# Attention loads moved from ScalarE to SyncE, through DRAM tables laid out in the projections

## The reference

```
k_rows = lax.dynamic_slice_in_dim(kg, rs, kh, axis=1)[:, :, col_idx]   # 8 rows x 32 columns
bias   = jnp.take(bias_c, dr_idx, axis=1)                              # relative position, per head
s_loc  = einsum('bjqhd,bijkhd->bhjqik', q_r, k_rows) + bias            # NEG_BIG outside the window
s_ctx  = einsum('bjqhd,bmhd->bhjqm', q_r, ctx_k)                       # 256 cached context keys
p      = softmax(concatenate([s_loc, s_ctx], axis=-1))
o      = einsum(p_loc, v_rows) + einsum(p_ctx, ctx_v)
```

## Time and profile before

| what | value |
|---|---|
| device time, three runs | 3695.7, 3701.32, 3702.32 us, median 3701.32 |
| profiled execution | 3698.1 us, span 3696.4 us |
| granted clock of TensorE, mean over the span | 0.866 |
| busy TensorE, weight loads | 3125.3 us, 2724.5 us |
| busy VectorE, ScalarE, GpSimd | 1934.6, 1164.2, 654.8 us |
| DMA | 497.80 MB, mean 135 GB/s |

### The profile page before, as it was taken

The page is one execution under the profiler, slowest core; times in us unless marked ns, Lnnn a source line. Parts: engine busy times, 40 slices in busy tenths (PEclk is TensorE's granted clock), DMA queues, the critical chain, the costliest instruction groups (busy, mean ns, idle before and its releaser), DMA issues. The chain is left out here.

```text
span 3696.4 us, 52649 instructions
## 1 busy us (share of the span) xinstructions
PE 3125.3 (85%) x19831; PEld 2724.5 (74%) x19831; DVE 1934.6 (52%) x4013; ACT 1164.2 (31%) x2012; POOL 654.8 (18%) x900
## 2 busy tenths in 40 slices
PE   8679999975887788898689942999999999999990
PEld 1367788864666677787568832999999999999990
DVE  3531213224444488788534457566666566666644
ACT  0531224311333322222123301344444444444422
POOL 3013400014444100022101100012111111211102
PEclk9689999996889766557689955999999999999995
DMA  7334522216777210111133323556655555665528
GB/s 273 127 109 149 172 73 89 76 57 140 151 158 153 89 51 29 52 44 37 42 103 116 113 115 105 171 181 185 197 175 180 183 183 183 185 197 175 177 81 313
DMA packets 350119, 497.80 MB, mean 135 GB/s; under 512 B 98403, under 2 KB 239755, under 8 KB 348397
## 3 DMA queue, kind: packets, MB, share of 16 engines
q1 hardware_dynamic: 251615, 376.04, 31.2%
q0 software_dynamic: 24336, 85.48, 8.2%
q10 hardware_dynamic: 74000, 34.10, 4.5%
HBM read 387.07 MB, written 108.72 MB: 134 GB/s over the span
## 5 line engine op out<-in xcount | busy, mean ns | idle before, releaser
L2463 DVE TENSOR_TENSOR ex_wlow<-ex_w,ex_whigh 128x2048 fp32r<-128x2048 f32 x192 | 440.1, 2292 | 159.3 <-ACT ex_whigh L2403 159.1
L2403 ACT ACTIVATE ex_whigh<-ex_w 128x2048 fp32r<-128x2048 f32 x192 | 367.0, 1912 | 253.5 <-DMA ex_w<-in_w_up 142.0
L2291 PE MATMUL ex_Y<-ex_hs_high,ex_whigh 128*128 128x272 f32 x1024 | 302.2, 295 | 17.1 <-DVE ex_hs_low L2479 17.1
L2291 PE MATMUL ex_G<-ex_xs_high,ex_whigh 128*128 128x272 f32 x1024 | 300.9, 294 | 2.7 <-DVE ex_xs_low L2447 2.7
L2293 PE MATMUL ex_G<-ex_xs_high,ex_wlow 128*128 128x272 f32 x1024 | 297.1, 290 | 0.0
L2291 PE MATMUL ex_U<-ex_xs_high,ex_whigh 128*128 128x272 f32 x1024 | 296.7, 290 | 0.0
L2293 PE MATMUL ex_Y<-ex_hs_high,ex_wlow 128*128 128x272 f32 x1024 | 296.4, 289 | 0.0
L2293 PE MATMUL ex_U<-ex_xs_high,ex_wlow 128*128 128x272 f32 x1024 | 296.4, 289 | 0.0
L2292 PE MATMUL ex_G<-ex_xs_low,ex_whigh 128*128 128x272 f32 x1024 | 295.2, 288 | 0.0
L2292 PE MATMUL ex_U<-ex_xs_low,ex_whigh 128*128 128x272 f32 x1024 | 294.8, 288 | 0.0
L2292 PE MATMUL ex_Y<-ex_hs_low,ex_whigh 128*128 128x272 f32 x1024 | 294.6, 288 | 0.0
(11 more groups left out here) (361 smaller groups left out, 7749.7 us busy)
## 6 DMA issues: line engine op xcount, KB each, us to landing
ex_w<-in_w_gate SPq DMA_DIRECT2D x64, 1024.0 KB
ex_w<-in_w_up SPq DMA_DIRECT2D x64, 1024.0 KB
ex_w<-in_w_down SPq DMA_DIRECT2D x64, 1024.0 KB
wada<-in_ada_w SPq DMA_DIRECT2D x12, 2048.0 KB, 8.2
hg_rows<-hg_pool_rows SPq DMA_DIRECT2D x68, 256.0 KB, 3.0
at_k_high<-key_parts SPq DMA_DIRECT2D x64, 256.0 KB, 4.1
hg_pool_rows<-hp_res POOLq DMA_DIRECT2D x34, 384.0 KB, 2.8
hp_w<-in_w_in SPq DMA_DIRECT2D x48, 256.0 KB
```

The source lines that it names most:

```text
L2291: nc.tensor.matmul(out, wh, xh, start=start, stop=False)
L2403: nc.scalar.activation(h, v, ACT.Copy).then_inc(s_high, 1)
L2463: nc.vector.tensor_tensor(l, v, h, ALU.subtract).then_inc(s_low, 1)
```

## The change

In the projections, the padded bias tables (one copy, 64 floats a row) go to DRAM, and ScalarE issues, in the last 16 steps, two DMAs a head from DRAM to DRAM that lay the bias out by partition: `bias_query_tiles` (128 by 1008 floats a head) and `bias_key_tiles` (128 by 736). The tables are turned round on the query side in place of the key side, and attention reads them with a negative step. SyncE copies the values from DRAM to DRAM, after the last weight load, into `value_tiles`: for each block of 16 columns its 32 key columns, in groups of 128 keys (8.4 MB in four DMAs).

In attention, the next head's loads are issued by SyncE in 10 DMAs in place of 35: queries and context keys at segment 0, values at segment 4, bias at segment 8. The loads of head 0 stand at the first steps of SyncE's loop (bias, then queries and context keys), its values and head 1's bias 14 steps later. The product with the values is 3 segments behind the scores, and the copy of a unit's output and the reciprocal come one and one segment later, at the unit's end + 4 and + 8.

```diff
+BIAS_Q_W, BIAS_K_W = 15 * 64 + 48, 11 * 64 + 32
...
@@ projections, SyncE
-                        for h in range(8):
-                            sp.dma_start(padq[SKEW_ROWS * (h % 4) + 4:SKEW_ROWS * (h % 4) + 19, h // 4, 16:47], a["na_rpb"][0, h]).then_inc(s_pin, 16)
+                        sp.dma_start(padk[:, 16:47], a["na_rpb"][0].rearrange("h r c -> (h r) c")).then_inc(s_pin, 16)
...
                     if x == 2 * KD:
...
-                            sp.dma_start(skew_q[i * HALF_ROWS:(i + 1) * HALF_ROWS, :].rearrange("q (c x) -> q c x", x=64),
-                                         padq[:, i, :].unsqueeze(1).to_broadcast([HALF_ROWS, Q_COLS, 64])).then_inc(s_skew, 16)
-                        sp.wait_ge(s_flip, 1)
-                        sp.dma_start(skew_k.rearrange("q (b x) -> q b x", x=64),
-                                     padk[:, :].unsqueeze(1).to_broadcast([8 * 15, K_COLS, 64])).then_inc(s_skew, 16)
+                            sp.dma_start(pads[0][i * HALF_ROWS:(i + 1) * HALF_ROWS, :], padq[:, i, :]).then_inc(s_skew, 16)
+                        sp.dma_start(pads[1], padk[:, :]).then_inc(s_skew, 16)
...
-                sp.wait_ge(s_skew, 48)
+                for b in range(2):
+                    sp.wait_ge(s_po[b], PO[S_ALL + b])
+                for j in range(JW):
+                    sp.dma_start(v_w[j].rearrange("g (r x) d -> g r (x d)", r=4),
+                                 v_d[0:N_LAT, :].rearrange("(g r x) d -> g r (x d)", r=4, x=GRID_W)
+                                 [:, :, C * KEY_START[j]:C * (KEY_START[j] + K_COLS)]).then_inc(s_vw, 16)
+                sp.wait_ge(s_vw, 16 * JW)
@@ projections, GpSimd
-                        nc.gpsimd.tensor_copy(padk[:, 16:47], padr[:, ::-1]).then_inc(s_flip, 1)
+                        nc.gpsimd.tensor_copy(padq[:, :, 16:47], padr[:, :, ::-1]).then_inc(s_flip, 1)
@@ projections, ScalarE
+                def bias_tables(h):
+                    act.wait_ge(s_skew, 48)
+                    first = pads[0][SKEW_ROWS * h, 0:1]
+                    act.dma_start(bias_q[h].rearrange("(r c) x -> r c x", c=Q_COLS),
+                                  bass.AP(first.tensor, first.offset, [[64, 8], [1, Q_COLS], [1, BIAS_Q_W]])).then_inc(s_tab, 16)
+                    first = pads[1][15 * h, 0:1]
+                    act.dma_start(bias_k[h].rearrange("(r c) x -> r c x", c=K_COLS),
+                                  bass.AP(first.tensor, first.offset, [[64, 4], [1, K_COLS], [1, BIAS_K_W]])).then_inc(s_tab, 16)
...
+                    if n >= M - 16 and n % 2 == 0:
+                        bias_tables((n - M + 16) // 2)
@@ attention, SyncE
-        LEAD, TURN = 8, 3
-        FIRST, END = -LEAD - 14, Z + 12
+        LEAD, TURN, PV_LAG = 8, 3, 3
+        FIRST, END = -LEAD - 14, Z + 14
...
-        EVAC_AT = {end(u) + 3: u for u in range(U)}
-        RECIP_AT = {end(u) + 7: u for u in range(U)}
+        EVAC_AT = {end(u) + PV_LAG + 1: u for u in range(U)}
+        RECIP_AT = {end(u) + PV_LAG + 5: u for u in range(U)}
...
+                def scores_side(h):
...
+                    if h >= 2:
+                        sp.wait_ge(s_st, PER_HEAD * (h - 1))
...
+                def bias_side(h):
+                    b = h % 2
+                    if h >= 2:
+                        sp.wait_ge(s_F, 3 * (h - 1))
+                        sp.wait_ge(s_T, h - 1)
+                    sp.dma_start(FR[:, b, :, :].rearrange("p k x -> p (k x)")[:, 0:BIAS_Q_W], bias_q[h]).then_inc(s_raw[b], 16)
+                    sp.dma_start(TR[:, b, :, :].rearrange("p k x -> p (k x)")[:, 0:BIAS_K_W], bias_k[h]).then_inc(s_raw[b], 16)
+                def value_side(h):
...
+                    if h >= 2:
+                        sp.wait_ge(s_pv, PER_HEAD * (h - 1))
+                    sp.dma_start(V[:, b, 0:32, 0:HD], v_w[:, :, :, c].rearrange("j g p d -> p (j g) d")).then_inc(s_v[b], 16)
+                    sp.dma_start(V[:, b, 32:34, 0:HD], a["cache_na_v"][0, 0, :, h, :].rearrange("(i p) d -> p i d", p=P)).then_inc(s_v[b], 16)
+                    sp.dma_start(V[:, b, 34, 0:HD], v_d[N_LAT:, c]).then_inc(s_v[b], 16)
...
+                    if z == FIRST:
+                        bias_side(0)
+                        scores_side(0)
+                    if z == -LEAD:
+                        value_side(0)
+                        bias_side(1)
                     if z in KEYS_AT:
                         local_keys(KEYS_AT[z])
+                    if at == 0 and 1 <= h + 1 < HEADS:
+                        scores_side(h + 1)
+                    if at == 4 and 1 <= h + 1 < HEADS:
+                        value_side(h + 1)
+                    if at == 8 and 2 <= h + 1 < HEADS:
+                        bias_side(h + 1)
@@ attention, TensorE
-                    if z - 2 in UNIT_AT:
-                        weighted(z - 2)
+                    if z - PV_LAG in UNIT_AT:
+                        weighted(z - PV_LAG)
@@ attention, ScalarE
-                    if at == 1 and 2 <= h + 1 < HEADS:
-                        load_scores_side(h + 1)
-                    if at == 4 and 2 <= h + 1 < HEADS:
-                        load_values(h + 1)
```

More of the change, by code:

```diff
@@ L461, in _, with projections @@
                     low_part(t)
-def projections(nc, g, a, out, q_d, k_d, v_d, hgp, skew_q, skew_k):
+def projections(nc, g, a, out, q_d, k_d, v_d, hgp, pads, bias_q, bias_k, v_w):
     C = 512
@@ L494, in projections @@
         padq = m.sb("hp_bias_q", [HALF_ROWS, 2, 64])
-        padr, padk = m.sb("hp_bias_r", [8 * 15, 31]), m.sb("hp_bias_k", [8 * 15, 64])
+        padr, padk = m.sb("hp_bias_r", [HALF_ROWS, 2, 31]), m.sb("hp_bias_k", [8 * 15, 64])
         s_pz, s_pin, s_skew = (m.sem("hp_" + x) for x in ("pad_zero", "pad_in", "skew"))
-        s_flip, s_low, s_ck = m.sem("hp_flip"), m.sem("hp_low"), m.sem("hp_ck")
+        s_flip, s_low, s_ck, s_tab, s_vw = (m.sem("hp_" + x) for x in ("flip", "low", "ck", "tab", "vw"))
         s_hn, s_mm, s_na, s_ex, s_ln = (m.sem("hp_" + x) for x in ("hn", "mm", "na", "ex", "ln"))
@@ L745, in _ @@
                     last.then_inc(s_sg, 1)
+                act.wait_ge(s_tab, 16 * 16)
             @block.vector
@@ L1249, with attention @@
 STRIP_ROWS = 8 + 12 + 11 + 11 + 7
-def attention(nc, g, a, out, skew_q, skew_k, q_d, k_d, v_d, sums_d):
+def attention(nc, g, a, out, bias_q, bias_k, q_d, k_d, v_d, v_w, sums_d):
     with Mem(nc) as m:
@@ L1385, in local_keys @@
                     sp.dma_start(KL[0:HD, key_slot(u), :].bitcast(F32), k_d[1, HD * h:HD * h + HD, cols]).then_inc(s_key[key_slot(u)], 16)
+                def scores_side(h):
+                    b, rows = h % 2, slice(HD * h, HD * h + HD)
+                    if h >= 2:
+                        sp.wait_ge(s_st, PER_HEAD * (h - 1))
+                    for i in range(2):
+                        r = slice(HD * i, HD * i + HD)
+                        sp.dma_start(Q2[r, b, :].bitcast(F32), q_d[i, rows, :]).then_inc(s_kq[b], 16)
+                        sp.dma_start(C2[r, b, :].bitcast(F32), k_d[0, rows, J_N * J_KEYS:]).then_inc(s_kq[b], 16)
+                    sp.dma_start(CL[0:HD, b, :].bitcast(F32), k_d[1, rows, J_N * J_KEYS:]).then_inc(s_kq[b], 16)
+                def bias_side(h):
[6 more added lines that the diff above has]
+                def value_side(h):
+                    b, c = h % 2, slice(HD * h, HD * h + HD)
+                    if h == 0:
+                        sp.wait_ge(s_one, 1)
+                    if h >= 2:
[3 more added lines that the diff above has]
+                    sp.dma_start(V[:, b, 34, 0:HD], v_d[N_LAT:, c]).then_inc(s_v[b], 16)
                 def sums_out(u):
@@ L1498, in build_k @@
                     for kind in range(3):
-                        last = nc.gpsimd.tensor_tensor(T1[:, kind, :, :], TR[:, b, :, KEY_SHIFT[kind]:KEY_SHIFT[kind] + Q_COLS],
+                        last = nc.gpsimd.tensor_tensor(T1[:, kind, :, :], TR[:, b, ::-1, 31 - KEY_SHIFT[kind]:15 - KEY_SHIFT[kind] if kind < 2 else None:-1],
                                                        col_k[:, kind, :].unsqueeze(1).to_broadcast([P, 12, Q_COLS]), ALU.add)
@@ L2575, in program @@
     gates = dram("gate_rows", [2, 2, D])
-    skew_q = dram("bias_by_query", [8 * SKEW_ROWS, 64 * Q_COLS])
-    skew_k = dram("bias_by_key", [8 * 15, 64 * K_COLS])
+    pads = dram("bias_by_query", [8 * SKEW_ROWS, 64]), dram("bias_by_key", [8 * 15, 64])
+    bias_q, bias_k = dram("bias_query_tiles", [8, P, BIAS_Q_W]), dram("bias_key_tiles", [8, P, BIAS_K_W])
+    v_w = dram("value_tiles", [4, 8, P, NA_W])
     sums_d = dram("softmax_scales", [2, 4, 512])
@@ L2593, in program @@
             norm_transpose(nc, g, a)
-            projections(nc, g, a, out, q_d, k_d, v_d, hgp, skew_q, skew_k)
+            projections(nc, g, a, out, q_d, k_d, v_d, hgp, pads, bias_q, bias_k, v_w)
         g.aff = m.sb("affinities", [P, TILES, E_N])
@@ L2599, in program @@
             g.mixA = mm.sb("mix_attention", [P, 4, N_TOK])
```

(2 more changed lines are left out.)

60 lines of the change are left out of this document (13 added, 47 removed).

## The result

The changed kernel takes 3710.8 us, the one before 3693.1 us (medians of 8 runs each); the ratio is 1.0046, 95% interval 1.0032 to 1.0060. It is 17 us slower, where 8 us faster was forecast, and lies just outside the range of 3650 to 3710 us. The profiled executions, with spans of 3710.9 and 3696.4 us, show where the 14.5 us between them lie. Attention begins 11.5 us earlier (814.37 against 825.85); from there to the first exponential it takes 36.8 us in place of 56.9, 20.1 less; head 0 is 1.5 us shorter. Then heads 1 to 6 take 336.6 us in place of 292.6: 56.1 us each against 48.8, 44.0 us lost. Head 7 takes 1.0 us more, and the stages after attention 2.6 us, which I did not follow.

A forecast was written before the change was run, and what follows sets the result against it. Attention was taken as bound by ScalarE's load issues (12.1 us a head), projections by TensorE. Start -20, projections -7, heads +19 gave -8 against the profiled 3698.1 us, so 3690 us; range 3650 to 3710.

The forecast's parts named there:

- The start: Start of attention: bias transfers go first, so query bias lands at about 834 and TensorE waits less; 20 us gained.
- The projections: Projections: smaller bias stores let the next weight load go some 10 us sooner, closing TensorE's hole; 7 us gained.
- The value copy: End of projections: the 8.4 MB DRAM-to-DRAM copy has 97 us and is taken as hidden; other end costs 76 us.
- The bias in the heads: Attention heads: bias issued at segment 8 delays GpSimd's key table, scaling and ScalarE's copy; lag 10.1, head 46.7 us.
- The queue in the heads: Attention heads, segment 4: sums wait behind values and query load on SyncE's queue; 5.2 us late, head 51.9 us.
- the 55 that the prediction named as a sign of being wrong: Attention heads: a head over 55 us, or one under 46, would show the forecast wrong; 51 to 53 would be right.
- the 12.6 us landing: Start of attention, profiled kernel: 128 KB query load behind 1.5 MB of keys, read as queueing; 2.4 us with queue empty.
- Rival 2: Attention heads: not faster, the bias lands later still, 12.6 us in place of 5.9; 3730 us, chance 0.16.
- Rivals 1 and 3: Heads: 1, queue costs little, 3659 to 3671 us, chance 0.24; 3, holes close with nothing in their place, 3607, chance 0.08.
- Rival 4: End of projections: the value copy outlasts them, costing up to 76 us; 3766 us, chance 0.03.
- The holes of 12.1 us a head on ScalarE: Attention heads 1 to 6: ScalarE issues the next head's loads; removing 35 issues removes 12.1 us a head.

The follow-up runs named there:

- the early bias alone: Changed kernel with the bias of head h+2 issued at segment 12 of head h, replacing that of head h+1 at segment 8: 3664.7 us, ratio 0.9919.
- the patient reciprocal: Changed kernel with bias issued earlier, loads spread on SyncE or moved to ScalarE, and reciprocal two segments later: 3637.0 or 3631.1 us (spread on ScalarE: 3630.0).

## Why the prediction was wrong, step by step

- **The start: right.** 20 us were forecast, 20.1 came; GpSimd had the query bias 14.8 us into the stage (14.6 forecast).
- **The projections: right in kind, 7 forecast, 11.5 measured.** The term counted the idle time of one window. The hole's cost goes on behind it: from 330 to 360 us the changed kernel does 146 products at a granted clock of 1.00 and the one before 105 at 0.83; the 41 products are 8.4 us at the changed kernel's pace. Another 7 products (1.4 us) are missing in the kernel before from 400 to 450 us.
- **The value copy: right.** It is hidden, with more than 50 us to spare.
- **The bias in the heads: right in mechanism, 2.4 us too dear.** GpSimd's order makes the wait, as two opposite edits show (earlier bias, or the tables later in GpSimd's program: 48.4 us a head each). Its share is 7.7 us a head; the step had 10.1.
- **The queue in the heads: the step that failed.** "A scale load, three value issues and a query load at 0.57 us each put the sums at about 10, landing at 12.2 if nothing stood in their way." They were issued at 17.9. First, the scale load, which this count has at 7.0, went out at 11.9 (1011.16): SyncE waits ahead of it for the store of an older unit's scales, which took 7.2 us behind the keys and the 1.4 MB of queries issued at segment 0. The count has no such wait and charges the queries nothing. Second, from the scale load to the sums' load it took 6.0 us in place of 2.9, since one of the three value issues held SyncE for 3.7 us. Then the sums landed in 2.9 us, where the prediction had 5.4 (from 10 to 15.4, behind the values in the queue). They were there at 20.8 in place of 15.4; without the values at 15.8 in place of 12.2.
- **The two errors in one number.** In the prediction's terms the queue costs 11.7 us a head (48.4 without the bias, against 36.65) in place of 5.2, and the bias 7.7 in place of 10.1. So the head of 51.9 us became 56.1, above the 55 that the prediction named as a sign of being wrong, and the queue was mis-sized by more than the head's length shows. Six times the 4.2 us are 25 us; the projections' extra gain of 4.5 us and some 2 us at other places make of -8 the +14.5 between the profiled executions.
- **What the step meant by "queue" fell too.** I took the 12.6 us landing as a wait behind earlier transfers of the same queue, and after the result I still expected 56 us less if the loads left it. They left, and 7 us came. Bytes on either queue delay the sums. The rule that I weighed there from the Trainium skill (DMA: Bandwidth & Descriptors, section Issuing engines are not separate DMA queues) was right about the engines; I read it as "no queueing", and it means that no choice of issuer avoids it. The 12.6 us row was not one of a single queue either: while it was on its way, from 830.76 to 843.36 in the kernel before, both queues were at work (packets, MB, share):

```profile
q1 hardware_dynamic: 648, 2.00, 73.0%
q10 hardware_dynamic: 606, 0.82, 32.4%
```

- **The rivals.** Rival 2, the bias later still, came nearest, but by its issue (22.8 us into the head, where 17.6 follow from the forecast), not by its landing (4.6 us). Rivals 1 and 3 expected the sums early; nothing of that came. Rival 4 fell with the hidden copy.
- **Where the expected gain went.** The holes of 12.1 us a head on ScalarE did close. But 11.7 us opened with the sums and 7.7 with the bias. With the early bias alone a head was back at 48.4 us; with the loads spread or moved as well it fell to 44.5 or 46.4, and with the patient reciprocal on top to 43.6 or 42.4 (42.3 with both).

## What to carry to other kernels

When loads move to an engine that also runs a round trip of short transfers, list everything issued ahead of each short transfer that can still be under way, in bytes, and charge the short one with it, whichever queue it is on; and list every wait and every slow issue that the issuing engine passes before it comes to the short one. Then ask what stands behind the wait in each engine's program: a late load cost 7.7 us a head behind one order and nothing behind another. Room in the schedule (a reciprocal two segments later) was worth 4.0 us a head with the loads in a row on ScalarE, more than the 2.0 that the other queue gave, and 0.9 with the loads spread; the next buffer in the chain then took over the wait.

## What the runs showed of the hardware that I had not expected

A 2 KB transfer on a queue with little in it took 8.0 us to land while another queue moved 1.1 MB in rows of 256 bytes: from 1007 to 1009 us that queue had 109.0% of the engines' time (packets overlap) and the short transfer's own 20.9%. The issue of a 64 KB load right behind such a value load (4096 rows) took its engine 3.72 us on SyncE and 3.61 us on ScalarE, where most other issues took about 0.6: an issue can hold its engine for as long as six others. Where the values were loaded in four parts, one in a segment, the issue of the same 64 KB load took 0.38 us on SyncE and 0.52 us on ScalarE:

```profile
1015.58 0.38 SPq L1453 DMA_DIRECT2D at_V<-in_cache_na_v  x1
...
1005.65 0.52 ACTq L1714 DMA_DIRECT2D at_V<-in_cache_na_v  x1
```
